# When the gathered expert rows are loaded and used in a fused diffusion layer: a new schedule of the gathers

## The chip, the core and the metric

The kernel runs on one core of a Trainium2 chip. The time is device time in microseconds. The kernel before ran three times: 3475.9, 3476.8 and 3479.0 us, median 3476.8.

## What is computed

One layer of a diffusion backbone over 512 latent tokens and 256 context tokens of width 2048, in fp32: a mixer (a bidirectional mLSTM and a convolution branch, with one projection in and one out), then an expert layer named PEER, then a final RMSNorm. The change lies in the PEER part:

```
q = (t @ w_query)                     # t: 512 x 2048; 8 heads, two halves of 128
s = q against sub_keys                # 128 scores per half
top 16 of each half, then top 16 of the 256 sums  -> 16 experts per head, softmax gate
act = gelu(t . u_emb[expert]) * gate  # 128 experts per token, of 16384
out = sum of act * v_emb[expert]
```

## The kernel before, in words

The 512 tokens are treated in two ways. For the first 352 (384 on the v side) the kernel computes all 16384 neurons densely: unit by unit, 128 neurons at a time, all of u_emb is multiplied with the tokens (128 units, numbered 0 to 127 here), GELU is applied, the results go to HBM; they are multiplied with a table of gates, and in 128 more units (128 to 255, "the sums") all of v_emb is multiplied with them. For the last 128 tokens, and on the u side for the 32 before them, it gathers just the rows that the experts name: an indirect DMA brings, for one slot, one row of u_emb (later of v_emb) of 2048 values to each of 128 partitions (1 MB). There are 162 such rows of the u kind (128 slots, 32 for the extra tokens, and two plain loads that put the tokens' own values in PSUM) and 128 of the v kind. On VectorE (DVE) `dot(n)` (L1890) multiplies row n of the u kind with the tokens and sums it up, in two instructions of L1908: 1920 columns with the tokens in PSUM, 128 with those in SBUF. `add_rows(n)` (L2131, its instruction is L2140) adds row n of the v kind, times its activation, to four PSUM banks.

Matmuls keep fp32 accuracy by splitting each operand in two parts, so each product is three matmuls (`mm3`, L2236). A unit's 1 MB of weights goes through this line: SP loads it to one of four places of `ring`; ScalarE (ACT) writes its rounded part to one of two places of `split` (L1201, in two halves); GpSimd (POOL) subtracts to get the rest (`rest_half`, L847, instruction L851, in two halves); TensorE (PE) uses both. POOL works one to two units ahead of TensorE.

The gathers are issued on POOL too (`gather_rows`, L861, L886), in the same order of instructions: behind the two halves of a unit's split come the gathers that stand in that unit. The list `ROW_UNIT` (L100 to L115) has for each row the unit in whose place DVE uses it, and in which POOL issues its gather, one unit earlier for rows of units 44 to 115. A gather needs a free buffer: three (rows_a, rows_b, rows_c) until the neuron units end, in turn; for v rows also two in x2_dense, a place in SBUF that holds the dense tokens' low parts until unit 127 is done. POOL waits there until the row that was in the buffer has been used. Rows stand so: one per unit in units 3 to 115 (the first 41 in units 3 to 43); two in 116 to 125; four in 126; one and two in turn in the sums up to 147, none where the unit's number is 7 mod 8; the v rows from 150 to 244, evenly spread, none where it is 7 mod 8.

DVE runs the search (top 16 of the scores, L1945) while TensorE is in units 3 to 35, with a dot after each part of it; the dots there follow DVE's own order and not the units. After the search come dots up to row 36, the softmax (L2013 to L2017, which waits for ACT's Exp, L1346), more dots. TensorE needs the softmax behind unit 40, to transpose the gates. In units 44 to 115 DVE makes one-hots for 16 groups per 12 units (L2031) and reduces gate tables (L2048); ACT stores a table of 4 MB behind every twelfth unit, the last behind unit 115.

The sums: every eight units use two groups of four blocks of neurons. SP loads a group's neurons and gates to `weigh` (L691, 1.5 MB) as soon as DVE's `rest_group` (a_split, L2088) has freed the place, and in the same queue, in order, the v weights (L685). DVE multiplies them (`weigh_group`, L2084), ACT rounds (`a_hi`, L1398), DVE takes the rest (`rest_group`); the first group of the next eight is weighed in the unit that is 5 mod 8 and split in the one that is 7 mod 8, the second weighed in 6 mod 8 and split in 0 mod 8. TensorE waits for a_split at the start of the units that are 0 and 1 mod 8. In each odd unit DVE adds three finished PSUM banks to the sums (`flush`, L2105, L2108), and TensorE waits for a free bank in the even ones. DVE's order in a unit is:

```
k == 7: rest_group;  k == 0: rest_group
flush_here(unit, 0);  k in (5, 6): weigh_group
dots of the unit;  flush_here(unit, 1);  add_rows of the unit;  flush_here(unit, 2)
```

Further loads stand by `T_UNIT` (L121), the unit of the last u row: four units behind it ACT issues the broadcasts of g_final_row and ga2 (2 MB).

## Time and profile before

| | |
|---|---|
| median of three runs | 3476.8 us |
| the profiled execution's own time | 3469.2 us |
| its span, first to last instruction | 3467.4 us |
| TensorE busy | 3346.2 us (97%) |
| DVE, POOL, ACT busy | 2315.1 us (67%), 1860.7 us (54%), 1181.3 us (34%) |
| moved by DMA | 912.5 MB, mean 263 GB/s |
| units 0 to 127 | 1263.2 to 2369.2 us |
| units 128 to 255 | 2369.2 to 3455 us |

The page of the profile lists busy time by engine, the chain of work that ended last, and the costliest groups of instructions; the trace can be asked for the waits of one engine, for windows, and for the instructions in order of time. Times in the trace are from the first instruction on.

### The profile page before, as it was taken

The numbers are of one execution on the slowest core, as the hardware profiler recorded it, in microseconds if no ns is written. First come the engines' busy times: TensorE is split into PE (matmuls) and PEld (weight loads), VectorE is DVE, ScalarE is ACT, GpSimd is POOL, SyncE is SP. The second block draws the span as 40 slices with busy tenths as digits, with TensorE's granted clock in tenths as the row PEclk, the third lists the DMA queues.
The fourth block names the chain that finished last, engine by engine and source line by source line (L and its number), as shares of the span: only waits on it lengthen the run. The fifth ranks groups of instructions, "written<-read, shape, count | busy, mean of one in ns | idle before, by whom it ended". The sixth has DMA issues, their size and how long they took to land.

```text
span 3467.4 us, 43973 instructions
## 1 busy us (share of the span) xinstructions
PE 3346.2 (97%) x16931; PEld 2882.5 (83%) x16931; DVE 2315.1 (67%) x3420; ACT 1181.3 (34%) x1635; POOL 1860.7 (54%) x938
## 2 busy tenths in 40 slices
PE   7999999999999999999999999998999999999998
PEld 3688888766888889999999999997777787878787
DVE  2388886746314749996777666777765666576566
ACT  3322211233223232223655555522322232223223
POOL 1310001214444446667666666667777877878775
PEclk8999999999999999999999999999999999999999
DMA  9655642655423337778677887799778888879883
GB/s 380 257 188 201 218 164 104 187 217 204 171 97 146 110 121 261 265 265 312 269 314 316 321 316 300 280 395 352 285 306 341 355 318 345 353 308 358 352 335 140
DMA packets 190047, 912.51 MB, mean 263 GB/s; under 512 B 17437, under 2 KB 78317, under 8 KB 98660
## 3 DMA queue, kind: packets, MB, share of 16 engines
q1 hardware_dynamic: 122160, 525.38, 41.0%
q0 software_dynamic: 43584, 316.80, 22.5%
q10 hardware_dynamic: 24180, 68.80, 5.2%
q8 instruction: 64, 1.05, 0.1%
q14 instruction: 59, 0.48, 0.0%
HBM read 839.43 MB, written 71.42 MB: 263 GB/s over the span
## 4 chain that ended last, share of the span: by engine, by line
PE 65%; DVE 15%; DMA 13%; POOL 3%; issue 2%; ACT 1%; SPq 0%; ACTq 0%; DVEq 0%; POOLq 0%
PE bank L2236 59%; DMA ring<-in_v_emb 7%; POOL split L851 2%; PE bank L2497 2%; DVE rows_c L1908 2%; DVE rows_a L1908 2%; DVE rows_b L1908 2%; DVE a_split L2088 1%; PE bank L2614 1%; DMA ring<-in_w_mod 1%; DMA rows_c<-in_u_rows,small 1%; DMA rows_b<-in_u_rows,small 1%; DVE b L1975 1%; PE bank L2471 1%; DMA rows_a<-in_v_rows,small 1%
## 5 line engine op out<-in xcount | busy, mean ns | idle before, releaser
L851 POOL TENSOR_TENSOR split<-ring,split 128x1024 fp32r<-128x1024 f32 x544 | 1330.2, 2459 | 580.3 <-ACT split L1201 578.0
L2236 PE MATMUL bank<-h_hi,split 128*128 128x352 f32 (+1 forms) x4608 | 1203.9, 338 | 34.4 <-POOL split L851 33.3
L2236 PE MATMUL bank<-split,a_split 128*128 128x512 f32 x4608 | 1058.9, 391 | 26.9 <-POOL split L851 17.0
L1201 ACT ACTIVATE split<-ring 128x1024 fp32r<-128x1024 f32 x544 | 570.6, 1058 | 1415.3 <-PE bank L2236 1105.4
L2236 PEld LDWEIGHTS bank<-split,a_split 128*128 128x128 f32 x4608 | 864.8, 188 | 220.7 <-POOL split L851 25.5
L2236 PEld LDWEIGHTS bank<-h_hi,split 128*128 128x128 f32 x4608 | 822.8, 189 | 64.0 <-POOL split L851 17.8
L2236 PE MATMUL bank<-h_lo,split 128*128 128x352 f32 (+1 forms) x2304 | 772.3, 335 | 0.0
L2236 PEld LDWEIGHTS bank<-h_lo,split 128*128 128x128 f32 x2304 | 436.4, 189 | 12.1
L2236 PE MATMUL bank<-hT_hi,w_hi 128*128 128x512 f32 (+1 forms) x768 | 289.4, 377 | 5.3 <-POOL ring_lo L771 2.2
L2236 PE MATMUL bank<-hT_lo,w_hi 128*128 128x512 f32 (+1 forms) x768 | 287.0, 374 | 0.0
L2236 PE MATMUL bank<-hT_hi,ring_lo 128*128 128x512 f32 (+1 forms) x704 | 260.4, 370 | 0.0
L771 POOL TENSOR_TENSOR ring_lo<-ring,w_hi 128x2048 fp32r<-128x2048 f32 x13 | 60.3, 4638 | 295.8 <-ACT w_hi L528 295.7
L2048 DVE TENSOR_REDUCE b<-bank 128x512 f32<-128x1024 f32 x96 | 117.0, 1219 | 145.9 <-PE bank L2614 145.6
L528 ACT ACTIVATE w_hi<-ring 128x2048 fp32r<-128x2048 f32 x44 | 84.3, 1917 | 343.6 <-PE bank L2236 326.7
L2140 DVE SCALAR_TENSOR_TENSOR bank<-x_dense,small,bank 128x2048 f32<-128x2048 f32 x51 | 120.0, 2354 | 96.1 <-DMA x_dense<-in_v_rows,small 95.5
L2236 PEld LDWEIGHTS bank<-hT_hi,w_hi 128*128 128x128 f32 x768 | 145.1, 189 | 41.0 <-issue 14.2
L2108 DVE TENSOR_TENSOR acc<-acc,bank 128x512 f32<-128x512 f32 x180 | 120.4, 681 | 78.1 <-PE bank L2236 72.0
L2236 PEld LDWEIGHTS bank<-hT_lo,w_hi 128*128 128x128 f32 x768 | 145.1, 189 | 24.7
L1626 DVE SCALAR_TENSOR_TENSOR top<-top,conv_col 128x512 f32<-128x512 f32 x240 | 161.7, 746 | 0.0
L2036 DVE SCALAR_TENSOR_TENSOR onehot<-bank,expT,tiny 128x256 fp32r<-128x256 f32 x384 | 157.9, 473 | 0.1
L2236 PEld LDWEIGHTS bank<-hT_hi,ring_lo 128*128 128x128 f32 x704 | 132.3, 188 | 23.5
L1908 DVE CUSTOM_DVE_ANT_0 rows_b<-bank,rows_b 128x1920 f32<-128x1920 f32 x54 | 116.2, 2152 | 45.7 <-DMA rows_b<-in_u_rows,small 45.4
(335 smaller groups left out, 4032.2 us busy)
## 6 DMA issues: line engine op xcount, KB each, us to landing
ring<-in_u_emb SPq DMA_DIRECT2D x128, 1024.0 KB, 4.8
ring<-in_v_emb SPq DMA_DIRECT2D x128, 1024.0 KB, 14.8
ring<-in_w_mod SPq DMA_DIRECT2D x48, 1024.0 KB, 8.8
ring<-in_w_in SPq DMA_DIRECT2D x44, 1024.0 KB, 5.1
ring<-in_w_mod SPq DMA_DIRECT2D x64, 512.0 KB, 4.6
neurons<-tiny ACTq DMA_DIRECT2D x128, 192.0 KB, 3.6
gate_table<-b ACTq DMA_DIRECT2D x6, 4096.0 KB, 15.0
weigh<-neurons SPq DMA_DIRECT2D x32, 768.0 KB, 10.5
```

Of the source, the lines that this page charges most:

```text
L528: nc.scalar.activation(weight_slot(r).bitcast(F32R), weight_words(r), ACT.Copy).then_inc(whi_made, 1)
L771: nc.gpsimd.tensor_tensor(weight_rest(r).bitcast(F32R), weight_words(r), weight_slot(r), op=ALU.subtract).then_inc(wsplit_made, 1)
L851: nc.gpsimd.tensor_tensor(split[:, r % 2, 1, at].bitcast(F32R), ring[:, r % 4, :, :].rearrange("p k n -> p (k n)")[:, at], split[:, r % 2, ...
L1201: nc.scalar.activation(split[:, q % 2, 0, at].bitcast(F32R), ring[:, q, :, :].rearrange("p k n -> p (k n)")[:, at], ACT.Copy)\
L1626: nc.vector.scalar_tensor_tensor(y, u, w, y, ALU.mult, ALU.add).then_inc(conv_step, 1)
L1908: last = nc.vector.tensor_tensor_reduce(out=rows, in0=h2_rows, in1=rows, scale=1.0, scalar=0.0, op0=ALU.mult, op1=ALU.add, accum_out=sums[ ...
L2036: last = nc.vector.scalar_tensor_tensor(onehot[:, grp % 2, s, 1:3, :].bitcast(F32R), iota_bank.unsqueeze(1).to_broadcast([P, 2, P]), expT[ ...
L2048: nc.vector.tensor_reduce(stage[:, :, at:at + 4].rearrange("p i t -> p t i"), parts, AX.X, ALU.add)\
L2108: nc.vector.tensor_tensor(part, part, src, ALU.add).then_inc(sum_free, 1)
L2140: nc.vector.scalar_tensor_tensor(sparse_bank, rows, act_s[:, m:m + 1], sparse_bank, ALU.mult, ALU.add)\
L2236: last = mm(out_, left[a].bitcast(F32R), right[b].bitcast(F32R), start=start and n == 0, stop=stop and n == 2)
L2497: last = mm(bank[:, 4 + n % 2, 0:HD + 1], probT[:, d, s, j * P:(j + 1) * P], v_aug[:, s, h, :], start=i == 0, stop=i == len(keys) - 1)
```

## The change

It rewrites the list of units. Rows per unit, before and after:

| units | before | after |
|---|---|---|
| 116 to 125 | 2 each | 1 in the even, 2 in the odd |
| 126, 127 | 4, 0 | 2, 0 |
| 128 to 135, 136 to 143 | 1 2 1 2 1 2 1 0 | 1 1 2 2 2 2 2 0 |
| 144 to 151 | 1 2 1 1 0 0, then v rows: 2 0 | 1 1 2 2 2 0 0 0 |
| from 152, every eight | 10 or 11 v rows, up to unit 244 | 1 1 2 2 2 2 2 0, up to unit 236 |

The first 41 rows are gathered one unit later than the unit that they stand in (`GATHER_UNIT`), as far as the order allows: three gathers then stand in unit 44. Buffers are given out by the longest unused one, and all five may be used from unit 131 on. In unit 126 DVE does the dots as weigh_group, dot, rest_group, weigh_group, rest_group, dot. The last u row stands in unit 148 instead of 147, so all that hangs on T_UNIT is a unit later. What is computed does not change.

```diff
--- before.py
+++ after.py
@@ -101,19 +101,39 @@
 
     at = list(range(3, PRE))
     for unit in range(PRE, NK - 2):
-        at += [unit] * (2 if unit >= PRE + CHUNKS * CHUNK_UNITS else 1)
-    at += [NK - 2] * 4
-    unit = NK
-    while len(at) < U_ROWS:
-        if unit % 8 != 7:
-            at += [unit] * min(1 + unit % 2, U_ROWS - len(at))
+        at += [unit] * (2 if unit >= PRE + CHUNKS * CHUNK_UNITS and unit % 2 else 1)
+    at += [NK - 2] * 2
+    unit, whole = NK, U_ROWS
+    while len(at) < ALL_ROWS:
+        at += [unit] * min((1, 1, 2, 2, 2, 2, 2, 0)[unit % 8], whole - len(at))
         unit += 1
-    units = [u for u in range(unit + 2, 2 * NK - 11) if u % 8 != 7]
-    return at + [units[m * len(units) // SLOTS] for m in range(SLOTS)]
+        if len(at) == whole and whole == U_ROWS:
+            unit, whole = unit + 2, ALL_ROWS
+    return at
+
+
+def row_places():
+
+    places, last = [], [-1] * 5
+    for n, unit in enumerate(ROW_UNIT):
+        place = min(range(5 if unit >= NK + 3 else 3), key=lambda b: last[b])
+        last[place] = n
+        places.append(place)
+    return places
+
+
+def gather_units():
+
+    at = []
+    for unit in ROW_UNIT:
+        shift = 1 if unit < PRE else -1 if unit < NK - 12 else 0
+        at.append(max(at[-1:] + [unit + shift]))
+    return at
 
 
 ROW_UNIT = row_units()
-ROW_PLACE = [n % 3 for n in range(U_ROWS)] + [(n - U_ROWS + 3) % 5 for n in range(U_ROWS, ALL_ROWS)]
+ROW_PLACE = row_places()
+GATHER_UNIT = gather_units()
 ROW_COUNT = [ROW_PLACE[:n + 1].count(ROW_PLACE[n]) for n in range(ALL_ROWS)]
 ROW_EARLIER = [max([m for m in range(n) if ROW_PLACE[m] == ROW_PLACE[n]], default=-1) for n in range(ALL_ROWS)]
 LANDED_EARLIER = (0, 0, 0, 64, 64)
@@ -872,7 +892,7 @@
                     pool.wait_ge(e_moved, 16 * (2 * EG + 1))
                 if n >= 3:
                     pool.wait_ge(rows_used, max(0, ROW_EARLIER[n]) + 1)
-                if n >= U_ROWS and ROW_COUNT[n] == 1:
+                if ROW_PLACE[n] > 2 and ROW_COUNT[n] == 1:
                     pool.wait_ge(split_used, 2 * V0)
                 rows, landed = gathered_rows[ROW_PLACE[n]], gathered[ROW_PLACE[n]]
                 if n in (E_LOAD, T_LOAD):
@@ -890,7 +910,7 @@
                 rest_half(r, 0)
                 rest_half(r, 1)
                 for n in range(ALL_ROWS):
-                    if U0 + ROW_UNIT[n] - (PRE <= ROW_UNIT[n] < NK - 12) == r:
+                    if U0 + GATHER_UNIT[n] == r:
                         gather_rows(n)
 
 
@@ -2147,12 +2167,10 @@
             first = ROW_UNIT.index(NK - 2)
             weigh_group(0)
             dot(first)
-            dot(first + 1)
             rest_group(0)
             weigh_group(1)
             rest_group(1)
-            dot(first + 2)
-            dot(first + 3)
+            dot(first + 1)
             for unit in range(NK):
                 g, k = unit // 8 * 2, unit % 8
                 if k == 7 and g + 2 < GROUPS:
```

## Rows read from the trace of the kernel before

**Rows 1.** The page: busy us of each engine, share of the span, instructions
```profile
PE 3346.2 (97%) x16931; PEld 2882.5 (83%) x16931; DVE 2315.1 (67%) x3420; ACT 1181.3 (34%) x1635; POOL 1860.7 (54%) x938
```

**Rows 2.** The page: the chain that ended last, by engine and line
```profile
PE bank L2236 59%; DMA ring<-in_v_emb 7%; POOL split L851 2%; PE bank L2497 2%; DVE rows_c L1908 2%; DVE rows_a L1908 2%; DVE rows_b L1908 2%; DVE a_split L2088 1%; PE bank L2614 1%; DMA ring<-in_w_mod 1%; DMA rows_c<-in_u_rows,small 1%; DMA rows_b<-in_u_rows,small 1%; DVE b L1975 1%; PE bank L2471 1%; DMA rows_a<-in_v_rows,small 1%
```

**Rows 3.** Windows, L2236 on PE alone: length, busy (matmuls), granted clock, DMA share, GB/s
```profile
1298.30:1361.50 63.20, 63.20 (x387) 1.00 0.78 283
...
1361.50:1604.20 242.70, 227.87 (x1346) 0.98 0.74 268
...
2251.30:2369.20 117.90, 99.44 (x578) 0.93 0.98 392
2369.20:2443.80 74.60, 68.15 (x291) 0.98 0.75 285
2443.80:2576.30 132.50, 131.76 (x577) 1.00 0.77 302
2576.30:2652.50 76.20, 68.48 (x289) 0.96 0.85 330
2652.50:3323.70 671.20, 659.44 (x2881) 1.00 0.86 341
...
2701.50:2711.50 10.00, 8.75 (x38) 1.00 0.77 320
...
3373.20:3438.50 65.30, 65.30 (x289) 1.00 0.44 170
```

**Rows 4.** Waits of POOL from 1361 to 1604 us: total, times, longest
```profile
POOL rows_b L886 <- DVE tiny L1908: 27.3, 9, 7.0
```

**Rows 5.** Timeline of DVE and ACT, 1599 to 1609 us: start, duration, engine, line, operation [idle before]
```profile
1599.64 2.16 DVE L1908 CUSTOM_DVE_ANT_0 rows_a<-bank,rows_a 128x1920 f32<-128x1920 f32 x1 [3.44 <-DMA rows_a<-in_u_rows,small]
...
1607.75 0.69 DVE L2013 TENSOR_REDUCE soft<-tiny 128x32 f32<-128x512 f32 x1 [3.65 <-ACT tiny L1346]
...
1608.86 0.69 DVE L2017 TENSOR_TENSOR tiny<-tiny,soft 128x512 f32<-128x512 f32 x1
...
1607.09 0.63 ACT L1346 ACTIVATE tiny<-tiny 128x512 f32<-128x512 f32 x1
```

**Rows 6.** Timeline of DVE and POOL at the change of stages
```profile
2274.31 2.16 DVE L1908 CUSTOM_DVE_ANT_0 rows_b<-bank,rows_b 128x1920 f32<-128x1920 f32 x1 [13.95 <-DMA rows_b<-in_u_rows,small]
...
2276.96 0.94 POOL L886 DMA_INDIRECT rows_b<-in_u_rows,small  x1 [12.92 <-DVE tiny L1908]
...
2356.38 0.94 POOL L886 DMA_INDIRECT rows_b<-in_u_rows,small  x1 [6.07 <-DVE tiny L1908]
```

**Rows 7.** Timeline of DVE in unit 134: the second instruction of two dots
```profile
2424.44 3.76 DVE L1908 CUSTOM_DVE_ANT_0 rows_a<-small,rows_a 128x128 f32<-128x128 f32 x1
...
2430.21 0.28 DVE L1908 CUSTOM_DVE_ANT_0 rows_b<-small,rows_b 128x128 f32<-128x128 f32 x1
```

**Rows 8.** Timeline of DVE in units 165 to 168
```profile
2696.81 2.36 DVE L2140 SCALAR_TENSOR_TENSOR bank<-rows_c,small,bank 128x2048 f32<-128x2048 f32 x1 [3.90 <-DMA rows_c<-in_v_rows,small]
2701.79 2.35 DVE L2140 SCALAR_TENSOR_TENSOR bank<-x_dense,small,bank 128x2048 f32<-128x2048 f32 x1 [2.63 <-DMA x_dense<-in_v_rows,small]
...
2707.90 0.68 DVE L2108 TENSOR_TENSOR acc<-acc,bank 128x512 f32<-128x512 f32 x1
...
2717.73 1.75 DVE L2088 TENSOR_TENSOR a_split<-weigh,a_split 128x1536 fp32r<-128x1536 f32 x1
...
2721.37 5.36 DVE L2088 TENSOR_TENSOR a_split<-weigh,a_split 128x1536 fp32r<-128x1536 f32 x1
```

**Rows 9.** Timeline of POOL in unit 168
```profile
2720.34 4.76 POOL L851 TENSOR_TENSOR split<-ring,split 128x1024 fp32r<-128x1024 f32 x2
```

**Rows 10.** Waits of SP's queue from 2576 to 3324 us: total, times, longest
```profile
SPq L692 <- DVE a_split L2088: 323.8, 22, 26.6
```

**Rows 11.** Timeline of ACT in units 153 to 155
```profile
2590.69 0.35 ACTq L1427 DMA_DIRECT2D g_final_row<-in_g_final  x1
...
2613.87 2.00 ACT L1201 ACTIVATE split<-ring 128x1024 fp32r<-128x1024 f32 x2 [17.50 <-DMA ring<-in_v_emb]
```

## The prediction

> **What bounds the kernel now.** I read the page's busy shares first, then the chain, then windows cut where units begin, then the timelines of the engines where a window was longer than its matmuls. TensorE is busy for 97% of the span [rows 1], and 59% of the chain that ended last is matmuls of L2236 [rows 2]. So only what holds up TensorE's units counts. A unit of the search and the neuron stage has 48 matmuls and takes 7.9 us when nothing disturbs it: 384 in 63.2 us. A unit of the sums has 36 and takes 8.16 us: 288 in 65.3 us [rows 3]. (The counts there are one to three higher, since a matmul that crosses an edge is counted.) Taking these costs off each window leaves what its waits cost, the excess [rows 3]:
>
> - units 12 to 39, under DVE's search: 242.7 - 28 x 7.9 = 21.8 us
> - units 116 to 127, the change of stages: 117.9 - 12 x 7.9 = 23.2 us
> - units 128 to 135: 74.6 - 65.3 = 9.3 us; units 136 to 151: 132.5 - 130.6 = 1.9 us
> - units 152 to 159: 76.2 - 65.3 = 10.9 us; units 160 to 239: 671.2 - 652.8 = 18.4 us, 1.8 per eight units
>
> All the change can win lies in these 85 us, 2.5% of the span.
>
> **The gathers of the search.** POOL issues the gather of row n behind its half of the split, and waits there for the dot of row n-3; the next split, which TensorE needs, is queued behind. For rows_b alone that wait stands 9 times, up to 7.0 us, and the other two buffers are alike [rows 4]. DVE is the slower side there, so the stall is the pace of the dots minus a slack of so many units. One unit later gives TensorE one unit of slack once: 7.9 us, no more; the DMA itself is not needed sooner, since DVE reaches each dot many microseconds after it landed. Two things take some back. The softmax must be done before TensorE's transposes behind unit 40, which begins at 1604.2 and will end at about 1604.2 itself. Row 36's dot starts at 1599.6, as before, since POOL is no earlier; it and its tail end at 1604.1, and the three softmax instructions, now not waiting for ACT's Exp (it can run a unit sooner than 1607.1), need some 1.8 us [rows 5]: done at 1605.9, a wait of 1.7 us. Then three gathers go out in unit 44, where one or two did; I give 0.4 us for one-hots that come late. Sum: -7.9 + 1.7 + 0.4 = **-5.8 us** (-8 to 0).
>
> **Fewer dots at the change of stages.** Units 116 to 125 had two dots each and unit 126 four; now one and two in turn, and two. The gather of row 115, issued beside the last table's 4 MB store, is waited for 13.9 us; POOL waits 12.9 us for its dot before gather 118, and 6.1 us before gather 136 in unit 126, with the splits of units 119 and 127 behind it [rows 6]. In the new order row 118 belongs to unit 119, row 136 to unit 132, so POOL is a unit ahead at the first and never meets the second. The late landing stays, so I keep 1.0 us at unit 119, and 2.0 us at unit 128 for a_split, which DVE makes between the dots of unit 126. Sum: 3.0 - 23.2 = **-20.2 us** (-23 to -12). Five buffers from unit 131 on instead of 150 only help POOL.
>
> **The u rows moved into the sums.** Of them 32 stand behind unit 127 instead of 25, two per unit in units 130 to 134, 138 to 142 and 146 to 148. In these odd units the dots stand before the flush that frees a PSUM bank, so a second dot in the even unit before pushes that flush. A dot's second instruction, 0.3 us alone, took 3.8 us while POOL split, after a first of 2.2 us [rows 5, 7]. A second dot so costs 2.4 to 6 us of DVE, less what it had idle for a landing there; I take +0.8 at unit 132, +2 at 134, +2.5 at 142 and 1.1 at 144, +1 at 148: **+7.4 us** (0 to +15).
>
> **The rows of the sums.** They had 11 adds per eight units, spread evenly; now 12: one in each of the first two units, two in the next five, none in the last. Each add is 2.35 us of DVE, and with two gathers in units 3 and 4 of the eight the second lands 5 us behind the first (2696.8 and 2701.8) [rows 8]. Unit 166 shows what that does: 38 matmuls took 10.0 us, 1.8 over, since DVE's flush came at 2707.9 [rows 3, 8]; a window of eight had this only where units 3 and 4 both had two, and now all have it. Then unit 5 gets a second add as well. In that window the half of a_split that the next eight units begin with started at 2717.7 and ended at 2719.5, when TensorE started unit 168 (2719.7). With one more add it ends at 2721.8: 2.1 us of wait [rows 8]. Against that, SP's next loads of weights and v rows wait for a_split (323.8 us in 22 waits), and behind them ring loads come late to ACT [rows 10]: fewer gathers beside them, and after a late start the second a_split is not behind a POOL split, so its loads go out earlier and the following eight are spared. So I take 4.4 us (1.8 + 2.1 + 0.5 of ring waits) and 0.5 us in turn, 2.45 on average: 9 x 2.45 = 22 for the windows from unit 160 to 231, 1 for the last. Units 152 to 159: one ring wait of ACT is 17.5 us, behind g_final_row's and ga2's broadcasts, issued at 2590.7 [rows 11]; they go out a unit later, behind the load that was late, and fewer gathers lie beside them. I take 10.9 - 5 + 2.1 = 8. Sum: 22 + 1 + 8 - 29.3 = **+1.7 us**; bounds -20 (nearly all ring waits gone) and +57 (the collision below in all windows).
>
> Here a rule bears. The second a_split of unit 168 began at 2721.37 and took 5.36 us against 1.75 alone; POOL's two splits had begun at 2720.34 and ended at 2725.10, and it ended 1.6 us later [rows 8, 9]. The Trainium skill ("SBUF — State Buffer", the section on its two separate sides) says that the pair of ports that VectorE and GpSimd share is held by whichever began first for its whole instruction. By that, DVE would get in after the first of POOL's two instructions; the trace shows it waiting for both. By the rule a collision would cost some 2.4 us less than the rival below counts.
>
> **Sum.** -5.8 - 20.2 + 7.4 + 1.7 = -16.9 us. The profiled execution had 3469.2 us (span 3467.4), so it would be 3452.3; its own time lies 7.6 under the median of the three runs, 3476.8, to which I add the same: 3459.9, say **3460**.
>
> **Rivals.**
> - The port collision (slower). If a_split for the next eight starts more than some 0.5 us after unit 0 began, POOL's split holds it, and it ends 7 us into the unit instead of 2.1: 5 us more. Row 8's start plus one add, 2720.1, is 0.4 us into unit 168, with POOL's splits at 2720.34: on the edge. In every second window (5) and at unit 144 that is +30: 3490; in all of them +55: 3515. For it: a_split was held this way for the second group almost every time. Against: after one late start DVE has room. Chance 0.32.
> - The ring waits go, and the a_split waits don't come, because landings are quicker with one gather at units 0 and 1: the sums cost 10 instead of 31: -21 more, 3439. Against: DVE has 24.5 us for units 5 to 7, and flushes, four adds, two weighings and a_split take 17 of them. Chance 0.13.
> - DMA as the bound. Eight new units carry 12 gathers, 8 ring loads and 3 MB of weights, 24.1 MB in 65.3 us, 369 GB/s; these units had 341. If that were a ceiling, eight units would take 70.7 us, 3.6 over their 67.1: 10 x 3.6 = +36 in place of my +1.7, 3494. But the change of stages ran at 392 GB/s [rows 3], so there is room. Chance 0.05. The Trainium skill ("HBM Reference", specifications) has 358 GB/s as a core's share of its pair's memory, by which the eight units would take 67.4 us; the 392 of this one core alone is above it.
> - The edit of the search doesn't do what it says because POOL waits for the same dots anyway: +6, 3466; inside my own case's range.
>
> **How the numbers follow.** My case has 0.50, with 3448 to 3472 for its own range; the rest as above. Below 3442 lies most of the second rival's half, above 3497 the worst of the collision; between them about 0.8. A measurement of this kernel tells 0.2%, 7 us, from no change. My case is faster in nearly all of it (0.46), the second rival all (0.13); the collision in every second window ends slower (0.27), with some same; DMA is slower. Faster 0.59, same 0.12, slower 0.29.
>
> **What would show it.** Right: POOL's waits for dots in units 12 to 39 shrink, and these 28 units take 235 us instead of 242.7; in its place a wait of 1 to 2 us at unit 40. No POOL wait over 6 us between units 117 and 127, and those twelve units take 98 us. In the sums, 1.9 us over at the sixth unit of most eights. Wrong: a_split (L2088, in the new numbering a few lines on) of 5 us at the start of a window with TensorE waiting for it, or units 128 to 151 costing over 25 us of excess.

## The result, and the profile of the changed kernel

The change made the kernel slower. Its median is 3486.4 us (nine runs, 3482.1 to 3496.9) against 3475.9 us of the kernel before beside it (nine runs, 3469.3 to 3479.0): a ratio of 1.0040, 95% interval 1.0029 to 1.0052. I had forecast 3460 us, 17 less than the 3476.8 of that time. The range, 3442 to 3497, held the result; the sign was wrong. That the range held it is no merit of the reasoning: two errors of opposite sign, below, partly made up for each other.

| | before | after |
|---|---|---|
| median of the runs together | 3475.9 us | 3486.4 us |
| span of the profiled execution | 3467.4 us | 3493.3 us |
| unit 0 begins | 1263.2 us | 1270.2 us |
| TensorE busy | 3346.2 us (97%) | 3359.8 us (96%) |
| DVE busy | 2315.1 us (67%) | 2262.7 us (65%) |
| mean granted clock of TensorE | 0.988 | 0.983 |

Of the 26 us between the spans 7 lie ahead of unit 0, where both kernels are the same. Unit 0 begins anywhere between 1259.4 and 1271.5 us in the profiles of this study, so this is chance, and only what lies behind it is compared below. There the profiles differ by 19 us, the medians by 10.5 and the ratio by 14: single executions differ by several us, the profile of the kernel before was one of its quick ones, and the windows below serve to say where, the ratios how much.

The same windows as in [rows 3], cut where the units of the changed kernel begin (length, TensorE busy with the matmuls of L2254, granted clock, DMA share, GB/s). They are units 12 to 39, 116 to 127, 128 to 135, 136 to 151, 152 to 159 and 160 to 239:

```profile
1368.50:1589.50 221.00, 221.00 (x1346) 1.00 0.76 291
2240.20:2336.90 96.70, 94.88 (x577) 1.00 1.00 397
2336.90:2419.40 82.50, 71.48 (x288) 0.94 0.72 277
2419.40:2567.90 148.50, 137.54 (x577) 0.95 0.77 302
2567.90:2644.00 76.10, 68.46 (x290) 0.95 0.87 348
2644.00:3350.10 706.10, 671.76 (x2880) 0.97 0.85 335
```

With the undisturbed costs of the prediction taken off (7.9 us per unit, 65.3 us per eight units of the sums), the excess of each stretch is:

| units | before | forecast | after |
|---|---|---|---|
| 12 to 39, the search | 21.8 | 13.9 | -0.2 |
| 40 to 43 (their length: 32.5, then 34.4) | | +1.7 | +1.9 |
| 116 to 127, change of stages | 23.2 | 3.0 | 1.9 |
| 128 to 151, u rows in the sums | 11.2 | 18.6 | 35.1 |
| 152 to 239, rows of the sums (v) | 29.3 | 31 | 64.1 |

So the first two edits won 41 us, 15 more than I had given them, and the rows of the sums lost 59 us where I had 9. Of the 59, 21 us are matmuls that took longer, at a granted clock of 0.94 to 0.97 where it had been 0.96 to 1.00: TensorE is busy for 949.2 us in the last four windows, and was for 927.8 [rows 3]. The rest is waiting.

**The search.** POOL's waits for the dots, 7.0 us each at worst before [rows 4], are gone but for 0.4 us for each buffer. What is left of POOL's waits in units 12 to 39, in part:

```profile
POOL split L871 <- ACT split L1221: 49.3, 50, 1.6
...
POOL rows_b L906 <- DVE tiny L1928: 0.4, 1, 0.4
```

And DVE itself is quicker, which I had excluded. Its instruction `b<-b,tiny`, of which the search has ten (line L1975 before, L1995 after; least, median and longest duration in ns):

```profile
L1975 DVE TENSOR_TENSOR b<-b,tiny x10: 691/5444/5499, 1299.6 to 1549.7; 128x512 f32<-128x512 f32 x10
```

```profile
L1995 DVE TENSOR_TENSOR b<-b,tiny x10: 691/2756/2761, 1306.7 to 1538.8; 128x512 f32<-128x512 f32 x10
```

The timelines of one of them, DVE and POOL, first before, then after, show why:

```profile
1452.26 5.49 DVE L1975 TENSOR_TENSOR b<-b,tiny 128x512 f32<-128x512 f32 x1
...
1451.29 1.16 POOL L886 DMA_INDIRECT rows_b<-in_u_rows,small  x1 [5.88 <-DVE tiny L1908]
1452.47 4.71 POOL L851 TENSOR_TENSOR split<-ring,split 128x1024 fp32r<-128x1024 f32 x2
```

```profile
1449.39 2.76 DVE L1995 TENSOR_TENSOR b<-b,tiny 128x512 f32<-128x512 f32 x1
...
1448.75 2.85 POOL L871 TENSOR_TENSOR split<-ring,split 128x1024 fp32r<-128x1024 f32 x1 [1.56 <-ACT split L1221]
1451.75 1.23 POOL L906 DMA_INDIRECT rows_b<-in_u_rows,small  x1 [0.15 <-issue]
```

Before, POOL had waited 5.88 us for the dot (it then issued the gather), so both halves of its next split were ready and ran back to back; DVE's instruction, which takes 0.69 us alone, ended 0.57 us behind the second (1457.75 against 1457.18). After, POOL is ahead of DVE and has one half at a time from ACT; DVE gets in behind that one half. Six instructions of this kind in units 12 to 39 took 5.4 to 5.5 us before, and five 2.76 us after; with others of the search they make up the difference. POOL's lateness made DVE late, and DVE's lateness POOL: a circle of two engines, as I read it, which one unit of slack opened.

**The rows of the sums.** TensorE's waits in units 160 to 239 (total, times, longest):

```profile
PE bank L2254 <- DVE a_split L2108: 32.7, 8, 4.1
PE bank L2254 <- DVE acc L2128: 5.7, 4, 1.7
```

The first did not exist before. DVE's timeline at the end of one group of eight, where unit 191 begins at 2916.2 and 192 should at 2924.4:

```profile
2905.98 2.35 DVE L2160 SCALAR_TENSOR_TENSOR bank<-rows_a,small,bank 128x2048 f32<-128x2048 f32 x1 [2.17 <-DMA rows_a<-in_v_rows,small]
...
2920.23 2.34 DVE L2160 SCALAR_TENSOR_TENSOR bank<-x_dense,small,bank 128x2048 f32<-128x2048 f32 x1
2922.67 2.35 DVE L2160 SCALAR_TENSOR_TENSOR bank<-rows_c,small,bank 128x2048 f32<-128x2048 f32 x1
2924.94 3.47 DVE L2108 TENSOR_TENSOR a_split<-weigh,a_split 128x1536 fp32r<-128x1536 f32 x1
...
2930.13 2.14 DVE L2108 TENSOR_TENSOR a_split<-weigh,a_split 128x1536 fp32r<-128x1536 f32 x1
```

The split that unit 192 begins with starts only at 2924.94 and ends at 2928.4, since the two adds of unit 190 stand ahead of it and run at 2920 to 2925, a unit late. From 2908 on DVE has no idle time, so it came to unit 190 late. Is that its own work, or what it waited for earlier? The windows of single units 184 to 192, all engines (busy of TensorE, its weight loads, DVE, ACT, POOL; then clock, DMA share, GB/s), point to the second as the start of it:

```profile
2857.40:2867.30 9.90, 9.90 (x37) 7.99 (x38) 5.86 (x5) 0.00 (x0) 4.27 (x2) 0.83 0.90 327
2867.30:2875.40 8.10, 8.10 (x37) 6.74 (x36) 3.17 (x3) 3.07 (x3) 6.16 (x4) 1.00 1.05 389
2875.40:2883.60 8.20, 8.20 (x37) 6.76 (x37) 1.07 (x2) 2.13 (x3) 7.15 (x5) 1.00 1.01 419
2883.60:2891.80 8.20, 8.20 (x38) 6.79 (x37) 5.54 (x4) 2.12 (x2) 6.65 (x4) 1.00 1.01 422
2891.80:2899.90 8.10, 8.10 (x37) 6.72 (x36) 4.03 (x3) 2.12 (x2) 6.67 (x4) 1.00 1.01 421
2899.90:2908.10 8.20, 8.20 (x38) 6.77 (x37) 6.03 (x4) 2.12 (x2) 6.65 (x4) 1.00 1.02 422
2908.10:2916.20 8.10, 8.10 (x37) 6.74 (x36) 8.00 (x6) 2.12 (x2) 6.28 (x2) 1.00 0.87 361
2916.20:2928.70 12.50, 8.41 (x38) 6.63 (x37) 12.40 (x7) 5.93 (x6) 10.93 (x5) 1.00 0.24 84
2928.70:2938.50 9.80, 9.80 (x36) 7.95 (x37) 5.83 (x5) 0.00 (x0) 4.25 (x2) 0.83 0.90 314
```

In units 186 to 189 the DMA queues move 419 to 422 GB/s at a share of 1, and no single unit that I cut has more than 423; DVE is busy for 1 to 6 of 8 us there, waiting for rows. In unit 191 the queues move 84 GB/s, and DVE is never idle. The mean over the stage, 335 GB/s, tells of neither. Units 184 and 192, behind a wait, show the other cost: their matmuls take 9.9 and 9.8 us at a clock of 0.83.

### The profile page after: what moved, and what is told of

Same layout as the page of the kernel before. It is cut to its first block, busy times and chain, and to the rows that moved or that the text cites. A ratio compares the mean times of both kernels' runs of the same rounds, so it can differ in the third digit from the quotient of the medians.

```text
span 3493.3 us, 43972 instructions
## 1 busy us (share of the span) xinstructions
PE 3359.8 (96%) x16931; PEld 2895.4 (83%) x16931; DVE 2262.7 (65%) x3420; ACT 1184.0 (34%) x1635; POOL 1872.3 (54%) x938
## 4 chain that ended last, share of the span: by engine, by line
PE 71%; DMA 12%; DVE 8%; POOL 4%; issue 3%; ACT 1%; ACTq 0%; SPq 0%; DVEq 0%; POOLq 0%
PE bank L2254 66%; POOL split L871 3%; DMA x_dense<-in_v_rows,small 2%; DMA ring<-in_v_emb 2%; PE bank L2515 2%; DMA ring<-in_w_mod 2%; DVE weigh L2104 2%; DVE bank L2160 1%; PE bank L2632 1%; DMA x_dense<-in_u_rows,small 1%; PE bank L2489 1%; DMA rows_c<-in_v_rows,small 1%; DMA rows_a<-in_u_rows,small 1%; DMA rows_a<-in_v_rows,small 1%; DVE a_split L2108 1%
## 5 line engine op out<-in xcount | busy, mean ns | idle before, releaser
L871 POOL TENSOR_TENSOR split<-ring,split 128x1024 fp32r<-128x1024 f32 x544 | 1361.0, 2512 | 674.8 <-ACT split L1221 672.9
L2254 PE MATMUL bank<-h_hi,split 128*128 128x352 f32 (+1 forms) x4608 | 1194.2, 337 | 1.1 <-DVE h_lo L1890 1.1
L2254 PE MATMUL bank<-split,a_split 128*128 128x512 f32 x4608 | 1080.0, 397 | 65.8 <-DVE a_split L2108 32.7
L2254 PEld LDWEIGHTS bank<-split,a_split 128*128 128x128 f32 x4608 | 882.3, 192 | 263.3 <-issue 41.9
L2254 PEld LDWEIGHTS bank<-h_hi,split 128*128 128x128 f32 x4608 | 817.1, 188 | 26.1 <-DVE h_lo L1890 1.3
L2254 PE MATMUL bank<-h_lo,split 128*128 128x352 f32 (+1 forms) x2304 | 769.1, 334 | 0.0
L2254 PEld LDWEIGHTS bank<-h_lo,split 128*128 128x128 f32 x2304 | 433.5, 188 | 12.0
L2254 PE MATMUL bank<-hT_hi,w_hi 128*128 128x512 f32 (+1 forms) x768 | 289.9, 378 | 5.3 <-POOL ring_lo L791 2.2
L2254 PE MATMUL bank<-hT_lo,w_hi 128*128 128x512 f32 (+1 forms) x768 | 287.6, 375 | 0.0
L2254 PE MATMUL bank<-hT_hi,ring_lo 128*128 128x512 f32 (+1 forms) x704 | 260.4, 370 | 0.0
L2254 PEld LDWEIGHTS bank<-hT_hi,w_hi 128*128 128x128 f32 x768 | 145.4, 189 | 41.0 <-issue 14.2
L2254 PEld LDWEIGHTS bank<-hT_lo,w_hi 128*128 128x128 f32 x768 | 145.4, 189 | 25.0
L2254 PEld LDWEIGHTS bank<-hT_hi,ring_lo 128*128 128x128 f32 x704 | 132.3, 188 | 23.4
L1928 DVE CUSTOM_DVE_ANT_0 rows_a<-bank,rows_a 128x1920 f32<-128x1920 f32 x48 | 103.3, 2152 | 54.3 <-DMA rows_a<-in_u_rows,small 54.0
```

Source lines behind the costliest of these rows:

```text
L871: nc.gpsimd.tensor_tensor(split[:, r % 2, 1, at].bitcast(F32R), ring[:, r % 4, :, :].rearrange("p k n -> p (k n)")[:, at], split[:, r % 2, ...
L1928: last = nc.vector.tensor_tensor_reduce(out=rows, in0=h2_rows, in1=rows, scale=1.0, scalar=0.0, op0=ALU.mult, op1=ALU.add, accum_out=sums[ ...
L2254: last = mm(out_, left[a].bitcast(F32R), right[b].bitcast(F32R), start=start and n == 0, stop=stop and n == 2)
```

## The experiments

Three theories stand in what was expected of the runs. **Theory 1**: DVE's own work (in the search, its lockstep with POOL) holds up TensorE. **Theory 2**: in the search, only my 5.8 us of slack; in the sums, gathered rows that land late because the queues are full. **Theory 3**: something else that came with the change, such as the places of the buffers or the load of the queues as a whole. All kernels were run beside the kernel before; "us" below is the ratio times 3474 us.

| kernel | ratio to before, 95% interval | us |
|---|---|---|
| the change | 1.0040, 1.0029 to 1.0052 | +14 |
| the shift of the search alone | 0.9957, 0.9942 to 0.9972 | -15 |
| the change without the shift | 1.0090, 1.0075 to 1.0106 | +31 |
| the change with v rows spread evenly | 0.9959, 0.9944 to 0.9974 | -14 |
| with u and v rows spread evenly | 0.9942, 0.9927 to 0.9958 | -20 |
| the change, adds of half the columns | 0.9976, 0.9963 to 0.9989 | -8 |
| the change, gathers of half the columns | 0.9848, 0.9826 to 0.9871 | -53 |
| the change, v rows 2 2 2 2 2 1 1 0 | 1.0130, 1.0111 to 1.0148 | +45 |
| even spreads, short shift | 0.9927, 0.9911 to 0.9943 | -25 |
| the same, v rows gathered a unit early | 0.9881, 0.9867 to 0.9896 | -41 |
| the same, u rows of the sums too | 0.9885, 0.9871 to 0.9900 | -40 |
| the change, v rows gathered a unit early | 1.0009, 0.9997 to 1.0020 | +3 |
| v rows early and over all units | 0.9870, 0.9853 to 0.9886 | -45 |

### The shift of the search

The first kernel keeps the rows of before, and takes from the change the function `gather_units` and this use of it:

```diff
-                    if U0 + ROW_UNIT[n] - (PRE <= ROW_UNIT[n] < NK - 12) == r:
+                    if U0 + GATHER_UNIT[n] == r:
```

> The kernel before with one part of the change: each gather of the search (rows that are dotted in units 3 to 39) is issued one unit later. Rows of the dots and everything else as before. Theory 1 (lockstep of POOL and VectorE): before, a dot that waited for its gathered row and POOL's next split, released by that dot, ran at the same time and shared a port, so the dots of the search took 86 us per ten instead of 79 and the matmuls waited; with the gathers one unit later all of the search's excess of about 22 us goes: some 3455 us, and the dot's second pass in the search (about 3.9 us each before) falls to about 2.2 us. Theory 2 (my prediction: only the waits at the rings and at the edges of the search go, the dot's own pace stays): 6 us, some 3470 us, dots as long as before.

The second takes it out of the change:

```diff
-        shift = 1 if unit < PRE else -1 if unit < NK - 12 else 0
+        shift = -1 if PRE <= unit < NK - 12 else 0
```

> The kernel after, with the gathers of the search back where they were before (the fewer dots at the change of stages and the pattern of the sums stay). Theory 1 (lockstep): units 3 to 39 take their 22 us of excess again, some 3508 us. Theory 2 (shift worth 6 us): some 3492 us. If the parts of the change don't touch each other, this kernel's distance to the changed one is that of the other kernel with the shift alone to the kernel before, with the sign turned.

Measured: 15 us gained alone, and 17 us lost when taken out (1.0090 against 1.0040). The two agree, so this part touches the others little. Both figures lie between the theories' totals, 22 and 6, so I go by the windows (with the shift alone: units 12 to 39, 116 to 127, 128 to 135, 136 to 151):

```profile
1369.60:1590.60 221.00, 221.00 (x1346) 1.00 0.76 291
2239.40:2358.80 119.40, 100.14 (x577) 0.93 0.98 387
2358.80:2431.40 72.60, 66.65 (x291) 1.00 0.76 290
2431.40:2567.40 136.00, 133.03 (x577) 0.99 0.75 296
```

The search's excess went whole, 21.7 us, as theory 1 had it, and some came back: 1.9 at unit 40, 1.5 in units 116 to 127 (117.9 before), 3.5 in 136 to 151 (132.5), with 2 less in 128 to 135. In the kernel without the shift units 12 to 39 have 20 us of excess again, and the slow instruction is back:

```profile
L1995 DVE TENSOR_TENSOR b<-b,tiny x10: 692/5438/5506, 1302.9 to 1552.9; 128x512 f32<-128x512 f32 x10
```

The shift alone makes it 2.76 us instead of 5.44. One sign that theory 1 named failed: the second instruction of a dot was to fall from some 3.9 to 2.2 us. Its longest fell, from 4.15 to 2.49, but its median rose from 0.3 to 1.5, and the 30 dots have no less of it in all. What got shorter are instructions of the search. That this comes of POOL's two halves running back to back is read from the timelines; I did not try it by itself.

### The patterns of the sums

The third kernel keeps all of the change but the pattern of the v rows; the fourth changes that of the u rows too.

```diff
-    unit, whole = NK, U_ROWS
-    while len(at) < ALL_ROWS:
-        at += [unit] * min((1, 1, 2, 2, 2, 2, 2, 0)[unit % 8], whole - len(at))
+    unit = NK
+    while len(at) < U_ROWS:
+        at += [unit] * min((1, 1, 2, 2, 2, 2, 2, 0)[unit % 8], U_ROWS - len(at))
...
+    units = [u for u in range(unit + 2, 2 * NK - 11) if u % 8 != 7]
+    at += [units[m * len(units) // SLOTS] for m in range(SLOTS)]
```

```diff
-        at += [unit] * min((1, 1, 2, 2, 2, 2, 2, 0)[unit % 8], U_ROWS - len(at))
+        at += [unit] * min((1, 2, 1, 2, 1, 2, 1, 0)[unit % 8], U_ROWS - len(at))
```

> The kernel after, with the last 128 rows of the sums (v rows) spread evenly over the units as the kernel before has them, in place of the pattern 1 1 2 2 2 2 2 0; shift, change of stages and the u rows by the pattern stay. Theory 1 (a run of 2 2 2 2 2 dots fills VectorE, so that its operand split for the next group of eight units is late by some 4 us, 8 times, and the rest of it by some 2 us): the 34 us that the v units lost come back: some 3452 us. Theory 3 (the loss is by other things that came with the change, such as the places of the buffers or the DMAs' load in all): within 10 us of the changed kernel, 3476 to 3486 us. My prediction on record gave the v pattern 1.7 us: some 3485 us.

> As the kernel with the v rows spread evenly, and the u rows in the sums too are not 1 1 2 2 2 2 2 0 but 1 2 1 2 1 2 1 0 over eight units (before: 1 2 1 2 1 2 1 0 as well, but with 20 rows left, where now 26 are). Theory 1: the 24 us that units 128 to 151 lost in the profile are the pattern's for the greater part, and of them some 15 come back: 3432 to 3442 us. If instead the greater number of rows behind the change of stages is what costs (26 in place of 20, with their loads), at most 5 us come back: 3447 to 3452 us.

Measured: without the v pattern the time falls from +14 to -14 us, so the new list of v rows cost 28 us. The even u rows give 6 us more. That is less than expected; in the profile units 128 to 151 win 21 us by it and units 152 to 159 win 11, but the v rows then begin at unit 156 instead of 152, stand closer, and units 160 to 239 lose 20. Here are these last units with the v rows even, first from 152, then from 156 (L2254 on PE):

```profile
2640.60:3317.20 676.60, 660.63 (x2881) 0.99 0.86 340
```

```profile
2610.40:3306.90 696.50, 667.53 (x2881) 0.99 0.86 340
```

Both are even; the first has 110 v rows there and an excess of 23.8 us, the second 115 and 43.7. The change has 116 and 53.3, the kernel before 108 and 18.4. So an even spread is the smaller part of what the third kernel won: it also put 11 rows into eight units instead of 12, and some 20 of the 30 us between it and the change go with five or six rows more. That is read from four kernels that differ in other ways too; no run changes the number alone. The new rule for the buffers, which both kept from the change, is out as the main cause; the load of the queues, which theory 3 named too, is not.

The fourth kernel, with 20 us less than before, has the three parts that help: shift, fewer dots at the change of stages, even rows. Against the shift alone the fewer dots brought 5 us in all. In the profile units 116 to 127 win 22 us and units 152 to 159 win 11, and 24 are given back in units 160 to 239, where the v rows stand closer because the seven moved u rows push them back.

### DVE's work or the landings

Two kernels halve one of the two suspects each. The first leaves out the second half of the sum over the v rows. The second fetches half a row in place of a whole one, and not the half that the sum needs.

```diff
-                nc.vector.scalar_tensor_tensor(sparse_bank, rows, act_s[:, m:m + 1], sparse_bank, ALU.mult, ALU.add)\
-                    .then_inc(rows_used, 1)
+                half = slice(0, 2)
+                nc.vector.scalar_tensor_tensor(sparse_bank[:, half, :], rows[:, half, :], act_s[:, m:m + 1],
+                                               sparse_bank[:, half, :], ALU.mult, ALU.add).then_inc(rows_used, 1)
```

> The kernel after, but the adds of the v rows take only the first 1024 of the 2048 columns (the second half of that sum is left out); gathers and their DMAs whole. Theory 1 (VectorE's own work of 12 adds in eight units is what makes its operand split for the next eight late): each add takes some 1.2 us in place of 2.35, 14 us less in eight units, the waits of TensorE for the split go and units 160 to 239 cost 10 us of excess or less in place of 52: some 3440 us. Theory 2 (the gathered rows land late, since 12 gathers in eight units fill the DMA queues, and VectorE is late because it waits for them in its fixed order): only the rest behind the last landing is shorter, at most 1.2 us per add; the waits shrink by a third to a half: some 3460 to 3470 us.

```diff
+                if n > U_ROWS:
+                    pool.indirect_dma_start(rows[:, 0:D // 2], None, v_rows[:, :].rearrange("r (h c) -> (r h) c", h=2),
+                                            bass.IndirectOffsetOnAxis(which, 0)).then_inc(landed, 16)
+                    return
```

> The kernel after, but the gathers of the v rows fetch 1024 of 2048 columns (another half row than the sum needs; the other half is left as it was), the adds whole. Theory 1 (VectorE's own work): landings are not what counts, the splits stay late by some 4 us every eight units and the time stays within 8 us of the changed kernel, some 3480 us. Theory 2 (late landings): a gather brings 0.5 MB in place of 1 MB, VectorE's waits for landings in the sums go, so do TensorE's waits for the split: some 3445 us or less.

Measured: half the adds, 1.3 us each, gave 22 us; half the bytes gave 67 us, with the adds whole. From issue to landing a gather took 12.3 us in the change and 7.0 us here (the x_dense rows, 1 MB and 0.5 MB; number, then median us):

```profile
x_dense<-in_v_rows,small POOLq DMA_INDIRECT x43, 12.3
```

```profile
x_dense<-in_v_rows,small POOLq DMA_INDIRECT x43, 7.0
```

Units 160 to 239 took 652.8 us with half the bytes, exactly the undisturbed 10 x 65.3, under the full work of 12 adds per eight units. So DVE's work, given rows in time, fits, and theory 1 is wrong for the sums in its strong form, that this work alone makes the split late. The run with half the adds is less one-sided than its total. TensorE's waits in its units 160 to 239:

```profile
PE bank L2255 <- DVE acc L2128: 17.6, 15, 1.9
...
PE bank L2255 <- DVE a_split L2108: 1.5, 7, 0.2
```

The waits for a_split are gone there as well, 1.5 us for 32.7; TensorE then waited for DVE's flush, which stands in the same fixed order, and 35 of the 53 us of excess stayed. DVE waited longer for the same landings (113.3 us for the x_dense rows alone, 72.1 in the change) and made up some of the lateness by working quicker behind them. So late rows and a full DVE act together, and the rows are the larger part. Half the bytes also relieve the loads of weights in the same queues; this run can't tell these from the gathers.

The pattern turned round, as many rows in eight units:

```diff
+        at += [unit] * min(((1, 1, 2, 2, 2, 2, 2, 0), (2, 2, 2, 2, 2, 1, 1, 0))[whole > U_ROWS][unit % 8], whole - len(at))
```

> The kernel after, with the v rows by the pattern 2 2 2 2 2 1 1 0 in place of 1 1 2 2 2 2 2 0: as many gathers, adds and bytes in eight units, only the two single ones stand in units 5 and 6, where VectorE also weighs the next group, and not in units 0 and 1. If the place of the rows decides: the split for the next eight units starts one add earlier per single unit (2.4 us each) and most of the 4.3 us per eight go, some 3460 us, though units 0 and 1 may now hold the second split. If 12 rows in eight units are too many in any order: within 5 us of the changed kernel.

It got worse, 1.0130, which neither side of my expectation had. Its wait is another one, ten times in units 160 to 239, and it falls in units 3 of the eights (units 184, 187 and 188):

```profile
PE bank L2254 <- POOL split L871: 57.8, 10, 6.6
```

```profile
2859.00:2867.10 8.10, 8.10 (x37) 6.72 (x36) 5.89 (x2) 3.07 (x3) 7.61 (x5) 1.00 1.05 410
...
2883.40:2897.20 13.80, 8.40 (x38) 6.61 (x37) 9.01 (x7) 3.08 (x4) 2.43 (x2) 0.99 1.03 412
2897.20:2907.00 9.80, 9.80 (x37) 7.94 (x38) 0.07 (x1) 1.99 (x2) 9.17 (x6) 0.84 0.95 385
```

ACT, which makes the other part of the split, had waited for a load of the ring in that unit:

```profile
2893.63 2.01 ACT L1221 ACTIVATE split<-ring 128x1024 fp32r<-128x1024 f32 x2 [17.09 <-DMA ring<-in_v_emb]
```

Over units 160 to 239 it waited 231.3 us for the ring, 132.7 in the change. The queues are full from unit 0 on, since the next weights are loaded there too. More gathers early delay the ring's loads, which reach ACT late, and through it POOL's split; more gathers late delay the rows themselves and DVE's split. So the same shortage shows at two places, and the pattern chooses which.

### Using the time in which the queues are idle

The short shift ends at the row of unit 33:

```diff
-        shift = 1 if unit < PRE else -1 if unit < NK - 12 else 0
+        shift = 1 if unit < PRE - 10 else -1 if PRE <= unit < NK - 12 else 0
```

> The kernel with even spreads of u and v rows (3453 us), with the search's gathers one unit later only up to the row of unit 33; the last ten rows (units 34 to 39) are gathered as before the change. The waits at units 40 and 45 (2.1 and 2.2 us in that kernel's profile) go, as units 40 to 44 have nothing new: 4 us less. If the lockstep of POOL and VectorE comes back in units 34 to 39 it takes 2 to 5 us again. Some 3450 us, range 3447 to 3455.

0.9927 against 0.9942: 5 us less by the ratios, but the two intervals overlap, so the time doesn't show a gain. In the profile the waits at units 40 and 45 are gone, and no lockstep returned in units 34 to 39.

If the shortage is one of full queues in units 0 to 5 beside empty ones in unit 7, a gather should go out earlier (here on the even spreads; the other kernel has the same `or len(at) >= U_ROWS` in the line of the change):

```diff
-        shift = 1 if unit < PRE - 10 else -1 if PRE <= unit < NK - 12 else 0
+        shift = 1 if unit < PRE - 10 else -1 if PRE <= unit < NK - 12 or len(at) >= U_ROWS else 0
```

> The kernel with the short shift and even spreads (3447 us), with every gather of a v row issued one unit earlier than the unit whose add uses it. Theory 2, as the traces now have it: in units 1 to 5 of each eight the DMA queues move some 420 GB/s, all they give, while in unit 7 they move nothing, and a gather issued there costs no one anything. The rows of units 0 and after land up to 8 us sooner, and of the 45 us that units 160 to 255 lose some 20 to 35 go: 3415 to 3430 us. If instead the queues are simply short of time over the whole eight units, the earlier gathers push the ring's loads back by as much as they gain: 3440 to 3455 us.

> The kernel after, whole, with nothing else changed than that each gather of a v row is issued one unit earlier. Theory 2: what was slow in the pattern is the landing of the rows of units 5 and 6, which VectorE waits for ahead of its split. They land a unit sooner here, so TensorE's waits for the split (32.7 us in 8 waits) go for the greater part: some 3450 to 3460 us, 30 less than the changed kernel. Theory 1 (VectorE's work alone): within 8 us of the changed kernel, 3480 to 3490 us.

Measured on the even spreads: 0.9881, 16 us less than 0.9927. The median, 3429.2 us, lies just inside what theory 2 gave; the gain lies below its 20 to 35. Units 189 to 192 show the queues at work in unit 191, where they had moved nothing, and nearly idle in unit 190 now:

```profile
2852.10:2860.20 8.10, 8.10 (x37) 6.72 (x36) 5.22 (x3) 2.12 (x2) 5.82 (x4) 1.00 1.01 422
2860.20:2868.40 8.20, 8.20 (x38) 6.78 (x37) 8.10 (x6) 2.13 (x2) 7.40 (x4) 1.00 0.29 90
2868.40:2876.50 8.10, 8.10 (x37) 6.74 (x36) 4.79 (x4) 3.50 (x3) 7.37 (x4) 1.00 0.85 306
2876.50:2884.70 8.20, 8.20 (x38) 6.76 (x37) 7.12 (x3) 2.50 (x3) 7.62 (x4) 1.00 1.05 410
```

On the change itself the same edit gave only 11 us, not 30. The mechanism was right: the waits of TensorE for a_split are gone altogether. The size was not, as the ring's loads now come late instead:

```profile
PE bank L2254 <- POOL split L871: 28.8, 20, 2.4
```

Two variants bring no more that can be told:

```diff
-        shift = 1 if unit < PRE - 10 else -1 if PRE <= unit < NK - 12 or len(at) >= U_ROWS else 0
+        shift = 1 if unit < PRE - 10 else -1 if PRE <= unit < NK - 12 or unit >= NK + 4 else 0
```

> As the kernel with the v rows gathered one unit earlier, and the u rows of the sums from unit 132 on too, where five buffers are free. The 15 us that units 128 to 151 lose shrink by some 5: 5 us under the kernel with the v rows alone. If the dots there are held by VectorE's own work and not by landings: no difference.

The u rows a unit early: 0.9885 against 0.9881, no difference; in the profile units 128 to 135 lost 5 us more and 136 to 151 one less.

```diff
-    units = [u for u in range(unit + 2, 2 * NK - 11) if u % 8 != 7]
+    units = range(unit + 2, 2 * NK - 11)
```

> The kernel with even spreads and the v rows gathered a unit early (3429 us), with the v rows over all units from 156 to 244, those of the last unit of each eight included, where no row stood in any kernel so far. Theory 2 (the queues' time, not VectorE's): in the profile of the kernel at 3429 us the DMA queues move 80 to 90 GB/s in unit 6 and 120 to 306 GB/s in unit 7 of each eight; a gather that now goes out in unit 6 is one less in units 0 to 5, where they move 420, so ring loads come sooner and of the 27 us that units 160 to 255 lose some 10 go: 3415 to 3425 us. Against it: in unit 0 the add of unit 7's row stands ahead of the second operand split in VectorE's order; if that decides, the split and the weights' loads behind it are late: no gain or up to 10 us slower, 3430 to 3440 us.

3427.6 us, 0.9870: not to be told from the 0.9881 of the even spread with early gathers. These two, at 3428 and 3429 us, and the one with the u rows early, which can't be told from them, are the fastest of the versions that compute the whole, 1.2 to 1.3% under the kernel before and 1.6 to 1.7% under the change.

## Why the prediction was wrong, point by point

The step that failed is the price of the rows moved into the sums, +7.4 and +1.7 us, where the profile has +24 and +35. It priced a further row by DVE's durations, took the landings as they were, and threw the queues out by an average. It also put at nothing what a wait does to the clock, 21 us of the 59. The forecast named one sign of being wrong that was met: units 128 to 151 cost 35 us, over its 25.

- **The gathers of the search** (forecast -5.8 us). The mechanism, slack for POOL, was right, and so was the new wait at unit 40 (1.9 us in units 40 to 43 for 1.7). The step "gives TensorE one unit of slack once: 7.9 us, no more" failed: it took the pace of the dots as DVE's own. That pace was set by POOL. DVE was busy for 237.7 of 242.7 us in units 12 to 39 before and for 206.0 of 221.0 us after, with the same work in them but for one dot. Measured: 21.8 + 0.2 - 1.9 = 20 us in the profile, 15 to 17 us in the medians. I had the duration in hand, 5.4 us where the same instruction takes 0.69 at its least.
- **Fewer dots at the change of stages** (-20.2): 1.9 us are left where I had 3.0. Right, mechanism and size, within these units. What the moved rows cost elsewhere is in the next two points.
- **The u rows in the sums** (+7.4, bounds 0 to +15): +24 in the profile, outside my bounds. I had costed each dot by DVE's durations and taken DVE's waits for landings as slack that new dots could fill. But the landings came later. In the change DVE waited 60 us for u rows in units 128 to 151, 30 before, of which the longest:

```profile
DVE x_dense L1928 <- DMA x_dense<-in_u_rows,small: 21.5, 7, 7.1
...
DVE rows_c L1928 <- DMA rows_c<-in_u_rows,small: 13.0, 4, 8.3
```

  The wait of 8.3 us ends in unit 133. Unit 134, right behind it, is the dearest of these units: 17.3 us for 8.2, with DVE busy throughout and the matmuls at a clock of 0.80:

```profile
2393.90:2411.20 17.30, 11.89 (x37) 8.86 (x36) 17.27 (x20) 2.12 (x2) 5.73 (x4) 0.80 0.57 238
```

  So lateness, DVE's work and the clock add up there. The run with even u rows took 21 us of the loss away; none separates the three.

- **The rows of the sums** (+1.7, bounds -20 to +57): +35 in the profile, 28 us by the run that takes the pattern out. The failing sentence is "the half of a_split that the next eight units begin with ... With one more add it ends at 2721.8: 2.1 us of wait": the wait was 4.1 us and came in eight of ten groups, since more than one add's time was added: the landings moved too, a collision with POOL stood in each wait (next point), and behind each wait the next unit took 1.7 us more at the lower clock, so that a late split cost 5.8 us for my 2.1. And I had every second group spared. A part of the loss goes with the number of rows, as said above.
- **The rival of the port collision** (3490 us, chance 0.32) named the right waiting instruction and nearly the right total. It was right in a smaller part: in each of the eight late groups the first a_split took 3.5 us for 1.75, since it started 0.5 us behind one of POOL's instructions. That is 1.7 of the 4.1 us of wait. The 5.4 us that it counted on never came (the second a_split takes 2.14), and the larger part is that the split started late. That the total was near is luck.
- **DMA as the bound** (chance 0.05) was thrown out by a comparison of averages: 369 GB/s wanted over eight units, 392 seen over twelve. That was true and beside the point. The need is not spread over the eight units: it was 402 to 421 GB/s in units 184 to 187 of the kernel before already, and 4 in unit 191. Here are its units 184, 187, 190 and 191, which I had not cut:

```profile
2852.50:2860.60 8.10, 8.10 (x37) 6.73 (x36) 5.89 (x2) 2.88 (x3) 7.55 (x4) 1.00 1.05 406
...
2876.90:2885.90 9.00, 8.40 (x38) 6.61 (x37) 5.17 (x4) 2.51 (x3) 2.47 (x2) 1.00 1.01 421
2903.30:2911.50 8.20, 8.20 (x38) 6.76 (x37) 8.20 (x6) 2.12 (x2) 6.19 (x3) 1.00 0.61 246
2911.50:2919.70 8.20, 8.20 (x38) 6.80 (x37) 7.82 (x5) 3.50 (x3) 7.44 (x4) 1.00 0.06 4
```

- What stays open: why the queues stand idle in unit 7. SyncE's queue waits for a_split (359.2 us in 22 waits in units 152 to 239, 323.8 before [rows 10]) with the ring's loads behind that wait in the same queue. That fits, but nothing was run to show it.

## What to carry to other kernels

Cut the DMA rate by the smallest unit of the schedule before calling a transfer free: a mean of 341 GB/s hid four units at 402 to 421 beside one at 4. Where an instruction's median is several times its minimum, as 5.44 to 0.69 us here, its time belongs to a neighbour, and a change of the neighbour's timing can give it back. When halving an engine's work gives 22 us and halving what it waits for gives 67, look at what it waits for first, but look also at which wait takes the place of the one that went. Both remedies helped here: fewer rows in eight units, evenly spread, by 28 us, and an earlier issue into the idle time by 11 to 16 us.

## What the runs showed of the hardware

- The queues of this core moved 419 to 423 GB/s in their busiest units, and no unit that was cut has more. In the sums of the change a 1 MB gather into x_dense took 12.3 us from issue to landing by the median (10.5 before the change). The Trainium skill ("DMA: Bandwidth & Descriptors", section on bandwidth) gives about the same for one core alone, 425 GB/s for large transfers. The windows above, of a core that ran alone, stand above the share of 358 GB/s that I cited ahead, which is therefore no ceiling here.
- In units 12 to 39 before the change six VectorE instructions with two operands in SBUF (L1975) start, by the trace, 0.2 us ahead of POOL's split, while POOL still issues a gather, and wait for both of POOL's instructions, which run back to back (5.4 to 5.5 us). After the change five start 0.2 to 0.6 us behind one and wait for that one (2.76 us). The others took 0.69 us with no split of POOL running. The Trainium skill ("SBUF — State Buffer", section on its two separate sides) says that the one that starts first holds the port pair. The five agree with it. By the starts that the trace records the six do not; but in unit 4 one that starts 0.01 us ahead of POOL's split takes 0.69 us, as the page would have it. What decides between these is not shown.
- A wait of TensorE of some 4 us cost more than itself: the next unit ran at a granted clock of 0.83 and took 9.9 and 9.8 us instead of 8.2 (units 184 and 192 above), some 1.7 us more. Behind the wait of 5.4 us in the turned pattern it was 0.84 and 9.8 us.
